# The end of an expert's body reordered: weights turned and taken ahead of the output, slot sums by columns, the next gather's second half behind them

## What is computed

```python
def moe_swiglu(h, w_r, w1e, w3e, w2e):
    logits = (h @ w_r).astype(jnp.float32)
    vals, idx = lax.top_k(logits, TOP_K)                  # 2 of 8 experts for a token
    wts = jax.nn.softmax(vals, axis=-1)
    comb = jnp.sum(jax.nn.one_hot(idx, N_EXPERTS, ...) * wts[..., None], axis=-2)
    out = jnp.zeros_like(h)
    for e in range(N_EXPERTS):                            # 8, each 1024 -> 3584 -> 1024
        out = out + comb[..., e:e + 1] * swiglu(h, w1e[e], w3e[e], w2e[e])
    return out
```

## Time and profile before

| | |
|---|---|
| time, median of 3 runs | 1824.28 us (1823.57 to 1831.66) |
| span of the profiled execution | 1820.4 us |
| median less span (what lies around the span) | 3.9 us |
| PE busy | 1665.7 us, 92% of the span |
| DVE, ACT busy | 953.5 us, 539.2 us |
| weights of the experts | 336 transfers of 1024 KB |
| first matmul of the experts' part to the end | 867.95 to 1820.4 us |

### The profile page before, as it was taken

One profiled execution on the slowest core, in us unless ns is written; L12 is line 12 of the kernel. 1 busy time (PEld: TensorE's weight loads), 2 busy tenths in 40 slices (PEclk: granted clock), 3 DMA queues, 4 the chain that ended last, 5 costly groups with the idle time before them and its releaser, 6 DMA issues. The chain is left out here.

```text
span 1820.4 us, 20735 instructions
## 1 busy us (share of the span) xinstructions
PE 1665.7 (92%) x8432; PEld 1132.1 (62%) x8432; DVE 953.5 (52%) x1320; ACT 539.2 (30%) x682; POOL 5.0 (0%) x14
## 2 busy tenths in 40 slices
PE   6999999999999999989899899978869999887877
PEld 3788666888888866977788687323238863332322
DVE  5578666444347766996787887101038851100102
ACT  5321336000000126245676675000017730000001
POOL 0000000000000000000000000000000000000000
PEclk9999999999999999999899999999899999899999
DMA  9320965222221353274899799799999979999997
GB/s 360 114 93 1 367 234 185 93 93 93 93 81 62 112 188 139 93 273 172 320 372 354 275 374 354 297 396 391 394 392 393 391 286 395 394 394 394 393 394 268
DMA packets 224119, 476.44 MB, mean 262 GB/s; under 512 B 10002, under 2 KB 33012, under 8 KB 223988
## 3 DMA queue, kind: packets, MB, share of 16 engines
q1 hardware_dynamic: 222176, 474.24, 71.1%
q10 hardware_dynamic: 1812, 0.41, 0.1%
HBM read 473.58 MB, written 1.05 MB: 261 GB/s over the span
## 5 line engine op out<-in xcount | busy, mean ns | idle before, releaser
L1132 PE MATMUL ps<-ring,work 128*64 128x512 f32 x1120 | 278.4, 646 | 63.4 <-DMA ring<-in_e_w 63.4
L2271 DVE TENSOR_TENSOR mixT<-work,ps 64x256 f32<-64x256 f32 x70 | 29.7, 424 | 433.6 <-ACT work L1635 432.5
L1132 PEld LDWEIGHTS ps<-ring,work 128*64 128x64 f32 x1120 | 87.5, 148 | 228.5 <-issue 228.4
L1760 DVE TENSOR_TENSOR ring_rounded<-ring,hT_rounded 128x2048 fp32r<-128x2048 f32 x84 | 191.7, 2288 | 28.1 <-ACT hT_rounded L1652 26.3
L782 PE MATMUL ps<-ring_rounded 128*128 128x512 f32 (+1 forms) x536 | 190.6, 356 | 2.9 <-DVE norms L2098 1.6
L1652 ACT CAST hT_rounded<-ring 128x2048 fp32r<-128x2048 f32 x84 | 159.8, 1910 | 43.3 <-PE ps L1205 22.0
L784 PE MATMUL ps<-ring_rounded 128*128 128x512 f32 (+1 forms) x472 | 163.3, 346 | 0.0
L784 PE MATMUL ps<-mixT_rounded,ring_rounded 128*128 128x512 f32 x328 | 127.6, 389 | 0.0
L1158 PE MATMUL ps<-ring,mixT 128*64 128x512 f32 x560 | 127.0, 594 | 0.4 <-DMA ring<-in_e_w 0.4
L783 PE MATMUL ps<-hT_rounded,work_rounded 128*128 128x512 f32 x304 | 118.3, 389 | 0.0
L782 PE MATMUL ps<-mixT_rounded,work_rounded 128*128 128x512 f32 x304 | 118.3, 389 | 0.0
(11 more groups left out here) (270 smaller groups left out, 2656.3 us busy)
## 6 DMA issues: line engine op xcount, KB each, us to landing
ring<-in_e_w SPq DMA_DIRECT2D x336, 1024.0 KB, 14.1
ring<-in_w_mod SPq DMA_DIRECT2D x24, 2048.0 KB, 11.1
ring<-in_w_in SPq DMA_DIRECT2D x12, 2048.0 KB, 8.9
ring<-in_w SPq DMA_DIRECT2D x22, 1024.0 KB, 8.0
ring<-in_w_out SPq DMA_DIRECT2D x4, 2048.0 KB, 15.3
ring<-in_w SPq DMA_DIRECT2D x4, 2048.0 KB, 7.8
ring<-in_w SPq DMA_DIRECT2D x2, 1536.0 KB, 9.7
mixT<-in_ctx SPq DMA_DIRECT2D x2, 512.0 KB, 4.1
```

The lines of the kernel that those rows point to most:

```text
L1132: ins = pe.matmul(acc[H * w:H * w + H, :], x[:, k, 0:H], piece_words(e, b, 2 * half + w)[:, kk * BLK:(kk + 1) * BLK], start=(k == 0), stop ...
L1760: return dve.tensor_tensor(dst, src, high, ALU.subtract)
L2271: dve.tensor_tensor(hid[H * q:H * q + H, b % 2, 0:256], esg[H:2 * H, b % 2, cols], ps[2 + b % 2][H:2 * H, cols], ALU.mult).then_inc(hid_re ...
```

## The change

On PE, the transposes of the next expert's weights go ahead of the last `down`. The four products of `add_slots` go by columns: (tile 0, half 0), (tile 1, half 0), (tile 0, half 1), (tile 1, half 1), where they went by tiles. The second half of the next expert's gather moves from the top of the loop, behind the jump out of the body and ahead of the count's load, to the end of `add_slots`, ahead of that jump. On DVE, taking the gather and the turned weights goes ahead of the copy of the output's second half, and the four additions follow the new order. At the end of the kernel ACT's squares and DVE's gate rows follow it too.

```diff
+SUMS = [(t, half) for half in range(2) for t in range(2)]
@@ PE add_slots
-                for t in range(TT):
-                    if t == 1 and e + 1 < NE:
+                for t, half in SUMS:
+                    if t == 0:
+                        pe.wait_ge(y_vector if half else y_scalar, STEPS * (e + 1))
+                    elif half == 1 and e + 1 < NE:
                         pe.wait_ge(swt_done, e + 2)
-                    for half in range(2):
-                        if t == 0:
-                            pe.wait_ge(y_vector if half else y_scalar, STEPS * (e + 1))
-                        for s in range(tiles):
-                            ins = pe.matmul(ps[(2, 3, 6, 7)[2 * t + half]][:], ...)
-                        ins.then_inc(sum_ready, 1)
+                    for s in range(tiles):
+                        ins = pe.matmul(ps[(2, 3, 6, 7)[2 * t + half]][:], ...)
+                    ins.then_inc(sum_ready, 1)
+                if e + 1 < NE:
+                    gather(e + 1, 1)
@@ PE few
                 down(NB - 2, (1,))
-                down(NB - 1).then_inc(y_ready, STEPS)
                 if e + 1 < NE:
                     turn_weights(e + 1)
+                down(NB - 1).then_inc(y_ready, STEPS)
@@ PE mid
                 down(NB - 2)
-                down(NB - 1)
                 if e + 1 < NE:
                     turn_weights(e + 1)
+                down(NB - 1)
@@ PE loop
             turn_weights(0)
+            gather(0, 1)
             for e in range(NE):
-                gather(e, 1)
                 chosen = pe.value_load(cnt_i[0:1, e:e + 1], min_val=0, max_val=SEQ)
@@ DVE few
                 if e + 1 < NE:
                     take_gather(e + 1)
+                    take_weights(e + 1)
                 dve.wait_ge(y_ready, STEPS * (e + 1))
                 dve.tensor_copy(yslot[H:2 * H, 0, 0:512], ps[0][H:2 * H, :]).then_inc(y_vector, STEPS)
-                if e + 1 < NE:
-                    take_weights(e + 1)
                 add_slots(e)
@@ DVE mid
-                dve.wait_ge(y_ready, STEPS * (e + 1))
-                dve.tensor_copy(yslot[:, 0, 512:1024], ps[1][:]).then_inc(y_vector, STEPS)
                 if e + 1 < NE:
                     take_gather(e + 1)
                     take_weights(e + 1)
+                dve.wait_ge(y_ready, STEPS * (e + 1))
+                dve.tensor_copy(yslot[:, 0, 512:1024], ps[1][:]).then_inc(y_vector, STEPS)
                 add_slots(e)
```

More of the change, by code:

```diff
@@ L1103, in add_slots @@
             def add_slots(e, y, w, tiles):
-                for t in range(TT):
-                    if t == 1 and e + 1 < NE:
+                for t, half in SUMS:
+                    if t == 0:
+                        pe.wait_ge(y_vector if half else y_scalar, STEPS * (e + 1))
+                    elif half == 1 and e + 1 < NE:
                         pe.wait_ge(swt_done, e + 2)
-                    for half in range(2):
-                        if t == 0:
-                            pe.wait_ge(y_vector if half else y_scalar, STEPS * (e + 1))
-                        for s in range(tiles):
-                            ins = pe.matmul(ps[(2, 3, 6, 7)[2 * t + half]][:], w(s, half)[:, t * P:(t + 1) * P],
-                                            y(s, half), start=(s == 0), stop=(s == tiles - 1))
-                        ins.then_inc(sum_ready, 1)
+                    for s in range(tiles):
+                        ins = pe.matmul(ps[(2, 3, 6, 7)[2 * t + half]][:], w(s, half)[:, t * P:(t + 1) * P],
+                                        y(s, half), start=(s == 0), stop=(s == tiles - 1))
+                    ins.then_inc(sum_ready, 1)
+                if e + 1 < NE:
+                    gather(e + 1, 1)
             def few(e):
@@ L1696, in _ @@
             act.preload_act_table_set(LOG_AND_EXP)
-            for i in range(4):
-                act.wait_ge(sum_done, 4 * (NE - 1) + i + 1)
-                act.activation(norms[:, i, :], yacc[:, i // 2, (i % 2) * 512:(i % 2 + 1) * 512], ACT.Square,
+            for n, (t, half) in enumerate(SUMS):
+                i = 2 * t + half
+                act.wait_ge(sum_done, 4 * (NE - 1) + n + 1)
+                act.activation(norms[:, i, :], yacc[:, t, half * 512:(half + 1) * 512], ACT.Square,
                                accum_out=token_sums[:, i:i + 1]).then_inc(squares_in, 1)
@@ L2248, in add_slots @@
             def add_slots(e):
-                for i in range(4):
-                    acc = ps[(2, 3, 6, 7)[i]]
+                for i, (t, half) in enumerate(SUMS):
+                    acc = ps[(2, 3, 6, 7)[2 * t + half]]
                     dve.wait_ge(sum_ready, 4 * e + i + 1)
-                    y = yacc[:, i // 2, (i % 2) * 512:(i % 2 + 1) * 512]
+                    y = yacc[:, t, half * 512:(half + 1) * 512]
                     dve.tensor_tensor(y, y, acc[:], ALU.add).then_inc(sum_done, 1)
@@ L2376, in gate_row @@
                 cols = slice((i % 2) * 512, (i % 2 + 1) * 512)
[L2377 removed]
+                dve.wait_ge(sum_done, 4 * (NE - 1) + SUMS.index((i // 2, i % 2)) + 1)
                 dve.tensor_tensor(osb[:, i // 2, cols].rearrange("p (k n) -> p k n", k=4),
```

1 line of the change is left out of this document (removed).

## The result

The changed kernel takes 1832.3 us (median of 20 runs, 1828.8 to 1837.6), the kernel before 1825.8 us in 20 runs beside it (1821.4 to 1831.7). The ratio is 1.0033 with a 95% interval of 1.0024 to 1.0041: 6.0 us slower, 4.4 to 7.5. The forecast was 1827 us, +2.55 us.

A forecast was written before the change was run, and what follows sets the result against it. Bound by the weights' transfers while `few` runs, by something else around `mid`, whose end pauses them. Terms +0.6 - 1.8 - 1.0 + 2.5 + 1.6 + 0.65 = +2.55 us on 1824.28 gave 1826.8, rounded to 1827; range 1817 to 1831.

The forecast's parts named there:

- the step on the jump's landing: At `mid`'s exits: a jump starting earlier still waits behind the same queued weights and lands no earlier; earlier start costed at 0.
- the base: Median of the kernel before, 1824.28 us, to which the summed terms were added.
- +0.6: At three boundaries behind `mid`: the last `down` ends 0.22 us later for the shifted transposes, +0.2 us each.
- -1.8: Boundary 1 to 2: without the gather behind the landing, `hidden` starts at about 1141.4 instead of 1143.19, -1.8 us.
- -1.0: Boundary 4 to 5: landing to `hidden` takes 0.95 us instead of 2.0, -1.0 us.
- the 0 at 3 to 4: Boundary from `few` to `mid`: the jump's start moves by no more than 0.3 us, both fetches slow; 0.
- The start of the jump: Exit of `mid`, expert 1: the jump starts once `y_vector`'s wait is met, at 1134.7 instead of 1136.6, 1.9 us earlier.
- The 0 at 0 to 1: Boundary into `mid`: the branch sets `hidden`'s start and covered the gather; jump and branch stay in a row; 0.
- The slow clock (+2.5, +0.8, +0.8): Idle time right ahead of `hidden` puts the slow clock on it: +2.5 us at 0 to 1, +0.8 at 1 to 2 and 4 to 5.
- The end (+0.65): Expert 7's last products: by columns neighbours share a half and overlap less, +0.65 us, bounds 0 and 1.5.
- A (the jump lands earlier): Rival, chance 0.25: at `mid`'s exits the weights do not hold the code's packet; jump takes 4.05 us; -5.65 us, 1818.6.
- B: Rival, chance 0.15: `hidden` of experts 1, 2 and 5 each runs 5.5 us at half speed; +6.4 us, 1830.7.

The follow-up runs named there:

- gather_back: Changed kernel with the second half of the next expert's gather back at the loop's top, behind the jump; 1.0003 of the kernel before, +0.5 us.
- hold_back: Changed kernel, gather's second half back at the loop's top; after `mid`, SP holds the last two pieces' transfers until PE enters the next body; 0.9964, -6.6 us against before.
- hold_back_2: Repeat on another occasion of the changed kernel with SP's hold on two transfers and the gather back at the loop's top; 0.9963, -6.8 us against before.
- few_early: Changed kernel with the gather's second half in `few` next to the first, ahead of the last two `down`; 1.0039, +7.1 us against the kernel before.
- gather_only: Kernel before with only the gather's second half moved from the loop's top to behind the four products; 1.0010, +1.8 us against the kernel before.
- warm: Changed kernel with three idle 128x512 products at the end of `mid`, behind the gather and ahead of the jump; 1.0026, +4.7 us against before.
- warm_same_size: Changed kernel with three idle products behind `mid`'s gather and three left out of the unused `big`, so bodies keep their places; 1.0018, +3.3 us against before.
- few_early_warm: Changed kernel with `few`'s second gather half next to its first and three idle products behind the gather in `mid`; 1.0022, +4.0 us against before.
- hold_after: Changed kernel with SP holding the last two pieces' transfers after `mid` until PE enters the next body; 1.0007, +1.3 us against the kernel before.

## Why the prediction was wrong

The sign, a change of less than 0.5% and the step on the jump's landing were right; the time lies 1.3 us above the range of 1817 to 1831. Of the 5.5 us between 1826.8 and 1832.3, 1.5 belong to the base and 4.0 to the sum (3.5 by the ratio).

The step that failed is the length of the pauses, the terms +0.6, -1.8 and -1.0 with the 0 at 3 to 4. They forecast -2.2 us in sum, and the profiles show +1.3: the gather's instructions hold back the jump out of `few`, and moving the gather ahead of the jump saves less behind the landing than was reckoned. That is 3.5 us. The clock was forecast at +4.1 us and counted at +4.5, but its three parts were off by -1.4, +0.4 and +1.5, so that the sum is right by luck. By stages, the forecast failed at experts 2, 4 and 5 (-0.8, 0 and 0, against +1.7, +1.3 and +2.9).

- **The base.** The sum was set on 1824.28; 20 runs of the same kernel gave 1825.76.
- **The landing (0, and +0.2 each).** That an earlier jump lands no earlier is right, and shown by `gather_back` (start 1.9 us earlier than before, landing 0.3 us later) and by `hold_back` (the weights away, landing 2.7 to 2.8 us sooner than in `gather_back`, 2.4 to 2.7 in `hold_back_2`). The +0.2 each for the shifted turn was +0.2, +0.5 and +0.7 in the mean of the profiles (+0.3 at the last without one landing of 8.65 us).
- **The start of the jump.** Forecast 1 us behind the first product, as soon as the wait for `y_vector` is met. It was 2.6 us, and `gather_back`, without the gather's 32 instructions in front of the jump, has 1.0. Harmless in `mid`, because the landing is fixed. The rule of 64 from the Trainium skill's page Advanced Engine Details and Errata (section Engine Queue Depths), set aside in the prediction, does not fit either: 48 in front are enough to make the jump wait.
- **3 to 4 (0).** Forecast: the jump moves by no more than 0.3 us. It moved by 1.5, for the gather's instructions, which the prediction put ahead of the jump only in time, not in the queue. The stage of expert 4 became 1.3 us longer, and `few_early`, which takes them away, has it back.
- **From landing to `hidden` (-1.8 and -1.0).** Mis-sized. The 0.95 us was taken up to the branch; behind it stand the body's own semaphore instructions, which the gather used to cover, and the four profiles give 1.36 to 1.45 us. With the later landing, the pauses changed by -0.9 and +0.1 us, where -1.6 and -0.8 were forecast. The 0 at 0 to 1, +0.2 with the turn, was +0.6.
- **The slow clock (+2.5, +0.8, +0.8).** At experts 2 and 5 too small: "after the change the same at most" as before, but the loss rose by 1.2 and 2.3 us. The idle time ahead of `hidden` was put at 2.2 and 2.4 us and is 2.9 to 4.7 us in all eight entries, by the landing and the 0.45 us behind it that the steps above missed, and by products that start right behind `down` (`hidden` to first product of expert 0 takes 121.9 us in both kernels), not 0.2 us later. At expert 1 the loss behind the change was as forecast (2.6), but the kernel before loses 1.5 there in the mean; one profile with a clock of 1.00 was taken for the rule, and the term is +1.1. What these losses cost is shown for expert 5 only.
- **The end (+0.65).** Wrong: 2.11 us before and after. Eight records of 64 rows take a quarter of a microsecond each in both orders, whether neighbours use the same half or not.
- **The rivals.** A (the jump lands earlier) is refuted. B was the right rival in kind: the slow clock falls on all three entries, at 2.6, 1.6 and 2.3 us instead of 2.7 each. It shares the forecast's error in the pauses (-2.8 and +0.6).

## What to carry to other kernels

A wait taken from an engine's path is worth little, here +0.5 us, if what ends the path is a transfer that queues behind other transfers; look for what stands in that queue, and hold back what has time. Instructions put ahead of a jump can hold it back by standing in the engine's queue, even where the array has time for them. Work that runs behind a stall can take the slow clock on itself, so moving it ahead of the stall hands the slow clock to what follows. And one profile is one draw: the clock's share has to be read from several before a term rests on it, and a tally that meets the measured time can still have its shares wrong; a stage's whole length is the better test.

## What was not expected of the hardware

- The same jump takes 3.3 to 4.1 us with a weight queue that is empty or nearly so, 4.3 to 6.4 us with one that runs out meanwhile, and 6.1 to 6.4 us with a full one; a branch into the second body 3.9 to 4.6 and 6.3 to 7.0 us.
- Where nothing stands between landing and `hidden`, ten entries of experts 2 and 5 came behind idle times of 0.6 to 2.4 us (`gather_only`, `warm`, `warm_same_size`, `few_early_warm`, `hold_after`): the clock granted was full in nine and slow in one, behind 2.17 us. Ten entries came behind 2.9 to 4.7 us (the changed kernel and `few_early`), and all ten were slow, which means 1.2 GHz, the lower of the two levels. The idle time just ahead does not decide alone: at expert 1, where the gather stands between two idle times, the last was 3.48 us in `hold_back` with a clock of 1.00, and 2.08 us in the second profile of before with 0.75.
- Straight code can stop as well: 0.91 us with empty queues, 5.2 us with full ones. In `warm` the stop went when each body was put back to its place; the other cases were not tested.
